# First in-projection of an attention and Fourier encoder on one Trainium2 core: weight blocks split by other engines, a shorter lead, an early table load

## The reference

```python
# layer 0: differential attention, layer 1: Fourier mixing; x is (1, S, 1024)
h = rmsnorm(x, attn_norm)
proj = h @ attn_w_in                    # 1024 -> 4096
q, k, v, z = split(proj, 4)
...
x = x + (o * silu(z)) @ attn_w_out
h = rmsnorm(x, fnet_norm)
u, z = split(h @ fnet_w_in, 2)
...
x = x + (f * silu(z)) @ fnet_w_out
y = rmsnorm(x, final_norm)
```

## Time and profile before

| | us |
|---|---|
| median of 3 runs | 3069.11 (3066.42 to 3069.58) |
| the profiled execution, its own time | 3063.98 |
| its span | 3062.3 |
| PE busy | 2948.3 (96%) |
| DVE, ACT, POOL busy | 1474.1, 1348.6, 789.8 |
| first stage, PE busy of the first 34 us | 14.0 |

### The profile page before, as it was taken

The page is one execution under the profiler, slowest core; times in us unless marked ns, Lnnn a source line. Parts: engine busy times, 40 slices in busy tenths (PEclk is TensorE's granted clock), DMA queues, the critical chain, the costliest instruction groups (busy, mean ns, idle before and its releaser), DMA issues. The chain is left out here.

```text
span 3062.3 us, 41858 instructions
## 1 busy us (share of the span) xinstructions
PE 2948.3 (96%) x15110; PEld 2471.7 (81%) x15110; DVE 1474.1 (48%) x1688; ACT 1348.6 (44%) x2356; POOL 789.8 (26%) x414
## 2 busy tenths in 40 slices
PE   7999999999989999999999999998999899999899
PEld 6888888888868787878787878886688899887687
DVE  5111100000078787878787878787876200441322
ACT  6111111111167777767777777775443321321321
POOL 6211111111012222222222222223664320130642
PEclk8999999999989999999999999999999999999899
DMA  6333332242155413122223232121664522565752
GB/s 211 131 118 115 117 106 67 70 115 67 60 127 164 104 37 91 51 71 68 72 63 79 63 78 63 33 90 47 205 206 154 195 91 76 140 179 179 261 185 97
DMA packets 225924, 340.37 MB, mean 111 GB/s; under 512 B 21835, under 2 KB 171659, under 8 KB 220252
## 3 DMA queue, kind: packets, MB, share of 16 engines
q1 hardware_dynamic: 221004, 321.10, 33.4%
q0 software_dynamic: 4736, 16.91, 2.0%
HBM read 224.68 MB, written 126.03 MB: 115 GB/s over the span
## 5 line engine op out<-in xcount | busy, mean ns | idle before, releaser
L1017 DVE TENSOR_REDUCE pa_half_max<-pa_score 128x1 f32<-128x1024 f32 x512 | 625.5, 1222 | 232.8 <-PE pa_score L805 232.8
L951 ACT ACTIVATE pa_p<-pa_score,pa_neg_max 128x1024 f32<-128x1024 f32 x512 | 568.2, 1112 | 73.7 <-DVE pa_neg_max L1023 70.2
L864 PE MATMUL pa_o_acc<-pa_wt,pa_vv 128*128 128x256 f32 x2048 | 510.9, 380 | 1.1 <-ACT pa_o_out_s L986 0.3
L1108 POOL TENSOR_SCALAR pa_p<-pa_p,pa_inv_sum,pa_lam_neg 128x2048 f32<-128x2048 f32 x128 | 262.9, 2054 | 947.0 <-DVE pa_inv_sum L1044 947.0
L801 PE MATMUL pa_score<-pa_ka,pa_qa 128*128 128x512 f32 x1024 | 454.9, 444 | 20.4 <-ACT pa_p L951 11.0
L206 PE MATMUL ia_acc<-ia_xh,ia_wh 128*128 128x512 f32 (+1 forms) x1280 | 471.9, 369 | 1.1 <-DVE ia_stage L505 1.1
L207 PE MATMUL ia_acc<-ia_xl,ia_wh 128*128 128x512 f32 (+1 forms) x1280 | 471.3, 368 | 0.0
L208 PE MATMUL ia_acc<-ia_xh,ia_wl 128*128 128x512 f32 (+1 forms) x1280 | 470.8, 368 | 0.0
L805 PE MATMUL pa_score<-pa_kb,pa_qb 96*128 96x512 f32 x1024 | 422.9, 413 | 0.0
L931 ACT ACTIVATE pa_wt<-pa_turned 128x512 f32<-128x512 f32 x512 | 306.3, 598 | 261.6 <-PE pa_turned L833 261.0
L864 PEld LDWEIGHTS pa_o_acc<-pa_wt,pa_vv 128*128 128x128 f32 x2048 | 366.9, 190 | 44.8 <-ACT pa_o_out_s L986 2.1
(11 more groups left out here) (270 smaller groups left out, 4260.1 us busy)
## 6 DMA issues: line engine op xcount, KB each, us to landing
ia_raw<-attn_w_in POOLq DMA_DIRECT2D x32, 512.0 KB, 4.7
qk_hi<-ia_stage SPq DMA_DIRECT2D x64, 256.0 KB, 2.0
qk_lo<-ia_stage SPq DMA_DIRECT2D x64, 256.0 KB, 2.1
pa_ka<-qk_hi SPq DMA_DIRECT2D x32, 512.0 KB, 6.7
fl_slices<-normed SPq DMA_DIRECT2D x26, 512.0 KB, 6.5
pa_vt<-v SPq DMA_DIRECT2D x8, 1152.0 KB, 6.3
x<-oa_x SPq DMA_DIRECT2D x18, 512.0 KB, 2.9
normed<-oa_h_out SPq DMA_DIRECT2D x9, 1024.0 KB, 5.4
```

What stands on the lines that cost most here:

```text
L864: mm = pe.matmul(o_acc[:], vv[:, k], wt[:, g % 2, k], start=k == 0, stop=k == NB - 1)
L951: act.activation(dst[:, half * HALF:(half + 1) * HALF], score[:, (4 * q + j) % RING].rearrange("p a b -> p (a b)"), ACT.Exp, bias=neg_max[ ...
L1017: dve.tensor_reduce(half_max[:, q % 2, n, half:half + 1], score[:, (4 * q + j) % RING].rearrange("p a b -> p (a b)"), AX_X, ALU.max).then_ ...
L1108: pool.tensor_scalar(p1[:, par], p1[:, par], inv_sum[:, par, 1:2], lam["neg"][:, 0:1], ALU.mult, ALU.mult).then_inc(p1_scaled, 1)
```

## The change

Four things in `project_resident`:

1. `EARLY` goes from 8 to 6: six tiles are turned before unit 0 rather than eight, and every interleaving of tiles with units on PE, ACT, DVE and SP shifts by two tiles.
2. The low parts of the first two weight blocks are subtracted by DVE (`weight_low`), the first right after `inverse(0)`, the second after the last turn of tiles ahead of unit 0's eviction. POOL keeps the two copies of the high part: the first ahead of `scale(0)`, the second after `scale(4)`.
3. POOL issues the load of the second weight block only when tile 1 of the tokens has landed.
4. ACT runs a square root on a constant as soon as the constant is set, ahead of the first tile.

```diff
-    EARLY = 8
+    EARLY = 6
...
+        ahead_in, table_in = m.sem("ahead_in"), m.sem("table_in")
...
-                for u in range(2):
-                    load(u, u)
+                load(0, 0)
+
+                pool.wait_ge(x_in[1], 16)
+                load(1, 1)
                 pool.wait_ge(consts_set, 2)
+                high(0, 0)
                 for t in range(NT + 3):
                     if t < NT:
                         scale(t)
-                    if 2 <= t < 6:
-                        (high, low)[t % 2](t // 2 - 1, t // 2 - 1)
+                    if t == 4:
+                        high(1, 1)
                     if t >= 3 and lo_of_pool(t - 3):
                         token_low(t - 3)
...
             def _(act):
                 act.wait_ge(consts_set, 2)
 
+                act.activation(root[:, 0:1], eps[:], ACT.Sqrt).then_inc(table_in, 1)
+                act.wait_ge(table_in, 1)
...
+                def weight_low(u):
+                    dve.wait_ge(w_hi, u + 1)
+                    dve.tensor_tensor(wl[:, u], raw[:, u], f32(wh[:, u]), ALU.subtract).then_inc(w_lo, 1)
...
                         for t in range(0 if n == 0 else EARLY + 2 * n, min(EARLY + 2 * n + 2, NT + 3)):
                             if t < NT:
                                 inverse(t)
+                            if t == 0:
+                                weight_low(0)
                             if 2 <= t < NT + 2:
                                 scale_columns(t - 2)
                             if t >= 3 and not lo_of_pool(t - 3):
                                 token_low(t - 3)
+                        if n == 0:
+                            weight_low(1)
```

More of the change, by code:

```diff
@@ L251, in project_resident @@
         copied, pool_held = m.sem("copied"), m.sem("pool_held")
-        ahead_in = m.sem("ahead_in")
+        ahead_in, table_in = m.sem("ahead_in"), m.sem("table_in")
         all_blocks = sum(n for n, _, _ in sections)
```

## The result

The changed kernel takes 3086.55 us (median of 4 runs, 3085.29 to 3090.09). The kernel before took 3069.35 in the same comparison (4 runs, 3066.42 to 3072.65): 17.2 us more, a ratio of 1.0056, 95% interval 1.0044 to 1.0068. It is slower by more than twice what the measurement can tell, which is about 0.2% as the prediction puts it.

The account below looks back on a forecast made before the run. It took PE as the bound, idling 20 us ahead of unit 0, then busy without waits past unit 9. Terms -6.5 + 1.7 + 15.6 + 7 = +17.8 gave 3081.8 profiled, median 3087 (5.1 added), range 3077 to 3095 us.

Parts of the forecast that it names:

- Part 3: PE waits for POOL's low parts in front of units 2, 4, 6 and 7; together +15.6 us.
- The chain of 5.84: From an eviction's start through ACT's square and root, DVE's reciprocal, POOL's scaling and subtract: 5.84 us, ahead of unit 2.
- Part 2: Two transposed tiles move from ahead of unit 0 to between units 5 and 6: +1.7 us.
- Part 1: The start: five edits together begin unit 0 6.5 us earlier, at about 27.5; bounds -9 and -3.5.
- The two tiles fewer: Ahead of unit 0: it could start at 29.51, once tile 3's low part is done, not 33.96; -4.4 us.
- The term "0" for the early root: At the start: tile 0's reciprocal is ready near 6.3, but POOL is busy or waiting until 10.3; gain 0.
- The terms for the split: At the start: block 0's subtract leaving POOL gives -2.1 us; block 1's no longer stretching DVE's subtract of tile 3, -2.0.
- Part 4: Matmuls behind the new gaps run at 1.2 GHz; three of four charged 2.3 each, +7 us, bounds 0 and 10.4.
- The clock holds: Rival: the four waits come, but the gaps are too short for the lower clock level; +10.8, 3080 us; chance 0.17.
- The start gains nothing: Rival: POOL waits for tile 1 and block 0, block 1 lands late; part 1 is 0, sum +24, 3093 us; chance 0.08.
- The waits don't come: Rival: POOL's low parts are ready in time, part 3's waits are absent; -4.8, 3064 us; chance 0.05.
- The fourth: Rival: POOL's turn-taking at the start is worth more; start gain 10, no clock loss, +7, 3076 us; chance 0.05.

Follow-up runs that it names:

- lead 8: The changed kernel with EARLY back at 8, everything else kept; median 3067.01 us, ratio 0.9989 to before.
- the lead alone: The kernel before with EARLY at 6 and nothing else changed; median 3089.28 us, ratio 1.0064 to before.
- lead 7: The changed kernel with EARLY at 7; median 3065.38 us, ratio 0.9984 to before.
- the run with the root alone: The kernel before with only ACT's early square root on a constant added; median 3070.06 us, ratio 1.0001 to before.
- the split alone: The kernel before with the two weight subtracts moved to DVE, POOL's copies, loads and lead of 8 kept; median 3065.01 us, ratio 0.9995 to before.
- Filling the gaps: The changed kernel with matmuls whose results are overwritten put in PE's gaps before units 2, 4, 6 and 7; median 3084.08 us, ratio 1.0049 to before.
- all low parts on DVE: The changed kernel with ALONE at 18, so DVE subtracts every tile's low part and POOL only scales; median 3087.85 us, ratio 1.0054 to before.

## Why the prediction was right

The median was forecast at 3087 and measured at 3086.55; the difference from before at +17.8, and measured at +17.2 in the medians, +20.5 in the trace of the stage, +23.6 between the two profiled executions. The mechanism was right term by term. That the median came within 0.5 us is luck. The same sum gave 3081.8 for the profiled execution, and that one took 3087.59, 5.8 more: 2.7 from the terms of the stage, as below, and 3.1 from the stages behind it. The 5.1 by which the median of before had stood above its profiled execution was added to the forecast; the change's median stands 1.0 below its own, and that made up for the rest. The terms, as the prediction put them:

**Part 3, the new waits (forecast 4.4, 4.4, 2.6, 4.2, sum 15.6).** Measured as PE's idle time 4.20, 4.34, 2.52, 4.25, sum 15.3. The chain of 5.84 was 5.76 behind unit 1. This step carries the result, and four runs hold it up: the waits go with the lead (lead 8), come with the lead alone, vanish with one tile more (lead 7), and follow DVE's duration when the subtract is moved there.

**Part 2, the moved pair of tiles (+1.7).** From the eviction-to-start distances, waits and pair together cost 17.9, forecast 17.3.

**Part 1, the start (forecast -6.5).** Measured -5.2. The sum was close, with terms that missed. The two tiles fewer (-4.4) measure -4.2 on the kernel before with the lead alone (29.78 against 33.96), and the edits to the start at a lead of 8 (-2.1 together) measure -2.5 (31.41); both at once give less than their sum of -6.7. Tile 1 was taken to land at 8.2; it landed at 9.91, the bound that I had named. So tile 0's scaling came at 12.20 rather than 10.3. Part of this was given back behind it: with tiles 2 and 3 already there, POOL scaled three tiles in one stretch of 3.54 from 14.63. The term "0" for the early root holds as far as the run with the root alone can tell. With POOL's first scaling freed as well, unit 0 started 1.8 earlier (27.25 against 29.08); that run also moved the second load, the first copy and DVE's subtract, so the share of the root is not shown. The terms for the split, -2.1 and -2.0, less 1.2 for DVE's own subtract on the path (which the run's expectation took and the prediction did not have), make 2.9; the split alone moved unit 0 by 2.0 with tile 1 landing 1.5 later, and by 2.8 against the kernel in which it landed alike.

**Part 4, the clock (forecast +7, three of four gaps at 2.3).** Measured on the units behind the four gaps: 1.6, 1.6, 0.1 and 2.4, and 0.3 in unit 8, 6.1 in all. Three long gaps charged, the short one not, as taken; the price was a little lower. Filling the gaps gives back 6.1 us at the end of the stage. The rule of the Trainium skill (TensorE: Matmul & The Clock Gate, Why this matters for your kernels), by which the long gaps are all charged, agrees with the three of 4.20, 4.34 and 4.25. A shorter gap was charged as well in another run (1.98 with all low parts on DVE, 1.7 lost), which length alone does not explain. The rest, 1.8, came in unit 0, which the prediction did not have: it ran at the lower level for longer than before (first matmul to eviction 7.96 against 6.15, at a granted clock of 0.70 against 0.93).

**The signs.** The list of waits came as written, in place and length, and ACT's one table load is over at 2.15. Three signs missed. POOL's first scaling came at 12.20 rather than 10.3. Unit 9's eviction starts 20.5 later (113.30 against 92.79), not 11 to 18. PE's waits for scaled tiles did not shrink to 14: they were 17.3, with 2.5 for tile 3's low part, 19.8 against 20.0 before. What got shorter ahead of unit 0 is PE's own turning, 8.8 us for six tiles against 14.0 for eight.

**Rivals.** "The clock holds" is out: it does not. "The start gains nothing" is out: 5.2. "The waits don't come" is out. The fourth needed a start gain of 10.

Together: the stage is 2.7 slower than forecast (20.5 against 17.8): 1.3 from part 1, 1.8 from unit 0's clock, 0.6 from parts 2 and 3, less 0.9 in part 4. In the medians this is not visible, within a scatter of 5 to 6 us.

## What to carry to other kernels

Where each engine's program is laid out by hand, shortening a lead moves work past the evictions on some engines and not on others. Before changing such a number, take each wait of the bounding engine and follow it back through the program order of every engine it passes: the question is behind which late event the last link stands, and the cost comes in a step (here 15 us for one tile of lead), not in proportion. And each long gap on PE cost more here than its length. Put the earliest possible work, not a wait for a transfer, at the head of a queue that feeds the critical chain.

## What the runs showed of the hardware

A shorter gap did not cost less clock. In the change the gap of 4.20 had a granted clock of 1.00 throughout, and the lower level came only after PE was at work again (0.77 over the unit behind it, 1.6 us lost). In the run with all low parts on DVE, the clock fell within the gaps of 2.96 and 2.91 (0.88 over each), and the units behind lost 2.9 each (8.61 and 8.62 against 5.74). Its gaps of 1.98 and 2.94 kept 1.00, and the units behind lost 1.7 (7.33 against 5.64) and 1.6 (4.63 against 3.07). The change's gap of 2.52 cost 0.1. So the loss behind one gap was anything from 0.1 to 2.9 us, and its size did not follow the gap's length in these runs. In these runs it went with when the clock fell. Where it had fallen well before PE was at work again (0.83 to 0.94 over the gap), 2.4 to 2.9 were lost; where the gap itself still had 0.99 or 1.00, it was 1.7 at most.

With both weight loads issued at once, tile 1's square, which waits for the tile to land, began at 10.17 to 11.36 in four profiles and at 9.83 in the one that the prediction used; in the seven profiles of kernels with the second load held back or issued behind the first scaling it began at 9.70 to 10.24. The prediction's 8.2 for one competing load was seen nowhere: with one block fewer in flight, tiles 2 and 3 came earlier, and tile 1 came more evenly rather than early.

DVE's first weight subtract took 2.29 (12.16 to 14.45) beside POOL's scaling of 1.19 at 12.20, against 1.22 undisturbed: it ended 1.06 behind POOL's end at 13.39, as if it had waited for POOL's whole instruction and then run. With the load not held back it went the other way round: the same subtract took 1.23 at 10.55, and POOL's scaling at 10.59 took 2.25, to 1.06 behind DVE's end. The Trainium skill (SBUF — State Buffer, section "SBUF: two separate sides") has this as an exclusive lock on the port pair that the two share, for a DVE instruction with two inputs in SBUF; the trace agrees.
